# A two-block transformer kernel: the first RMS norm summed in token columns, constants fetched ahead of the weights, and thirty products of zeros at the start

## What is computed

```python
def rms_norm(x, g):
    xf = x.astype(jnp.float32)
    y = xf * lax.rsqrt(jnp.mean(xf * xf, axis=-1, keepdims=True) + EPS)
    return (y * g.astype(jnp.float32)).astype(x.dtype)

def conv_mixers(h, w_in, ...):
    proj = jnp.einsum('bsd,dc->bsc', h, w_in)      # 1024 -> 7168 columns
    ...

x = x + conv_mixers(rms_norm(x, norm_mix_g[l]), w_in[l], ...)
mem_n = rms_norm(mem, norm_mem_g[l])
x = x + memory_cross_attention(rms_norm(x, norm_xa_g[l]), mem_n, ...)
x = x + peer_ffn(rms_norm(x, norm_peer_g[l]), ...)
```

## Time and profile before

| | before |
|---|---|
| time, median of 3 runs | 1473.1 us (1471.33 to 1473.85) |
| time of the profiled execution | 1473.38 us |
| span of the profiled execution (first to last instruction) | 1471.5 us |
| PE busy in the span | 1317.9 us (90%) |
| DVE busy | 955.8 us (65%) |
| ACT busy | 497.2 us (34%) |
| POOL busy | 496.9 us (34%) |
| bytes moved | 397.43 MB, mean 270 GB/s |

### The profile page before, as it was taken

How to read it: one execution, slowest core, us unless ns; L and a number is a source line. 1 busy time by engine, 2 the same in 40 slices (tenths; PEclk the granted TensorE clock), 3 DMA queues, 4 the chain that set the end, 5 groups by cost and what they waited for, 6 DMA issues and landing times.

```text
span 1471.5 us, 25626 instructions
## 1 busy us (share of the span) xinstructions
PE 1317.9 (90%) x9926; PEld 1253.8 (85%) x9926; DVE 955.8 (65%) x2100; ACT 497.2 (34%) x974; POOL 496.9 (34%) x334
## 2 busy tenths in 40 slices
PE   6999999999998886887878886888899999989997
PEld 5999999989888886887868886878776889889997
DVE  4679987665658685859585859655325447683574
ACT  4633456444133121212112121211236455434341
POOL 1588722000224554453535353555012000022221
PEclk9999999999999999898999898999999999999998
DMA  6555554553488999999999999999830125245451
GB/s 244 212 188 185 176 187 166 184 177 154 165 343 329 426 427 427 428 427 427 428 426 426 426 427 427 427 428 427 337 143 29 58 86 194 94 157 199 160 191 40
DMA packets 58090, 397.43 MB, mean 270 GB/s; under 512 B 6288, under 2 KB 9872, under 8 KB 10384
## 3 DMA queue, kind: packets, MB, share of 16 engines
q0 software_dynamic: 36864, 268.45, 43.6%
q1 hardware_dynamic: 21136, 127.76, 24.3%
HBM read 395.14 MB, written 1.05 MB: 269 GB/s over the span
## 4 chain that ended last, share of the span: by engine, by line
PE 55%; DMA 20%; DVE 14%; issue 7%; ACT 3%; POOL 1%; DVEq 0%; POOLq 0%; ACTq 0%
DMA rows_late<-peer_uv_dram,stage 20%; PE bank L721 10%; PE bank L723 10%; PE bank L722 10%; PE bank L963 7%; PE bank L689 6%; PE bank L707 5%; DVE rows_late L1990 4%; ACT w_hi L1165 2%; PE bank L838 1%; DVE w_lo L524 1%; DVE hid L2174 1%; PE bank L862 1%; DVE probs L1916 1%; DVE probs L1914 1%
## 5 line engine op out<-in xcount | busy, mean ns | idle before, releaser
L963 PE MATMUL bank<-h_norm,rows_late 128*128 128x128 f32 x2816 | 329.2, 280 | 24.8 <-ACT h_norm L1352 24.8
L963 PEld LDWEIGHTS bank<-h_norm,rows_late 128*128 128x128 f32 x2816 | 325.6, 196 | 27.8 <-ACT h_norm L1352 27.8
L524 POOL TENSOR_TENSOR w_lo<-raw,w_hi 128x2048 fp32r<-128x2048 f32 x37 | 172.1, 4652 | 392.7 <-ACT w_hi L1165 392.7
L1990 DVE SCALAR_TENSOR_TENSOR rows_late<-rows_late,squares 128x1024 f32<-128x1024 f32 x176 | 213.5, 1229 | 121.1 <-DMA rows_late<-peer_uv_dram,stage 120.6
L963 PE MATMUL bank<-h_norm,rows_early 128*128 128x128 f32 x1280 | 171.9, 300 | 84.7 <-ACT h_norm L1352 84.7
L963 PEld LDWEIGHTS bank<-h_norm,rows_early 128*128 128x128 f32 x1280 | 166.0, 214 | 90.6 <-ACT h_norm L1352 90.5
L631 POOL DMA_INDIRECT rows_late<-peer_uv_dram,stage x165 | 196.4, 1190 | 133.1 <-PE bank L963 94.5
L1165 ACT ACTIVATE w_hi<-raw 128x2048 fp32r<-128x2048 f32 x94 | 178.9, 1904 | 60.4 <-PE bank L723 49.4
L524 DVE TENSOR_TENSOR w_lo<-raw,w_hi 128x2048 fp32r<-128x2048 f32 x57 | 133.0, 2336 | 100.1 <-ACT w_hi L1165 96.5
L721 PE MATMUL bank<-x_hi_a,w_hi 128*128 128x256 f32 x672 | 190.9, 284 | 2.7 <-DVE x_lo_a L1560 1.8
L722 PE MATMUL bank<-x_lo_a,w_hi 128*128 128x256 f32 x672 | 190.2, 283 | 0.0
(11 more groups left out here) (338 smaller groups left out, 2036.5 us busy)
## 6 DMA issues: line engine op xcount, KB each, us to landing
raw<-w_in_dram SPq DMA_DIRECT2D x28, 1024.0 KB, 4.9
raw<-w_up_dram SPq DMA_DIRECT2D x16, 1024.0 KB, 4.9
raw<-w_down_dram SPq DMA_DIRECT2D x16, 1024.0 KB, 4.9
rows_late<-w_in_dram SPq DMA_DIRECT2D x10, 1024.0 KB, 13.4
raw<-w_kv_dram SPq DMA_DIRECT2D x8, 1024.0 KB, 4.8
rows_late<-w_peer_q_dram SPq DMA_DIRECT2D x5, 1024.0 KB, 12.0
raw<-sc_w_out_dram SPq DMA_DIRECT2D x4, 1024.0 KB, 4.8
raw<-cf_w_pw_dram SPq DMA_DIRECT2D x4, 1024.0 KB, 4.8
```

The source lines that it names most:

```text
L524: api.tensor_tensor(ring(w_lo, i), ring(raw, i), ring(w_hi, i).bitcast(F32), ALU.subtract).then_inc(w_lo_ready[LO_BY[i][0]], 1)
L963: mm = nc.tensor.matmul(ct(Y_ACC[c][t // 4], t % 4, P), expert_rows(k)[:, D + t * P:D + (t + 1) * P], ct(diag, k % DIAGS, P), start=False, ...
L1990: w_.scalar_tensor_tensor(out=row, in0=row, scalar=1.0, in1=h_tok[:, c * D:(c + 1) * D], op0=ALU.mult, op1=ALU.mult, accum_out=pre[:, side ...
```

## The change

Five edits, all at the front:

1. The norm "mix" joins `BY_TOKEN`, and its entry in `SUMMED` becomes 1: DVE adds nothing up, PE takes the 8 tiles of squares as they come, in 16 products with one moving column, and `spread("mix")` with its 2 products follows, behind a wait for the constants.
2. The constants are fetched ahead of weight block 0.
3. Weight block 2 is fetched directly behind block 1, ahead of the memory input, the positions and the subkeys.
4. PE begins with `WARM` = 30 products of `zeros` with `zeros`, as soon as POOL's second fill is done.
5. ACT takes a root of one number ahead of the squares, into a place that nothing reads.

The chain of DVE's seven additions for this norm is gone; the reciprocal of 128x256 becomes one of 128x2.

```diff
+WARM = 30
...
-BY_TOKEN = ("peer", "post_mix", "post_mlp")
-SUMMED = {name: DT - 2 if name in ("peer", "post_mix", "post_mlp") else DT for name, _ in NORMS if name != "mlp"}
+BY_TOKEN = ("mix", "peer", "post_mix", "post_mlp")
+SUMMED = {name: 1 if name == "mix" else DT - 2 if name in ("peer", "post_mix", "post_mlp") else DT for name, _ in NORMS if name != "mlp"}
...
             sp.dma_start(vec[:], T["vecs"]).then_inc(vec_landed, 16)
+            sp.dma_start(const[:], T["consts"]).then_inc(const_landed, 16)
             load(0)
             load(1)
-            sp.dma_start(const[:], T["consts"]).then_inc(const_landed, 16)
+            load(2)
...
-            for i in range(2, QUERIES[RING]):
+            for i in range(RING, QUERIES[RING]):
                 load(i)
...
                 for k in tiles:
-                    if k:
+                    if k or SUMMED[name] == 1:
                         pe.wait_ge(squared, square_count(name, k))
...
+            pe.wait_ge(filled, 2)
+            for _ in range(WARM):
+                nc.tensor.matmul(TAP_ACC[0][:, 0:P], zeros[:], zeros[:], start=True, stop=True)
             pe.wait_ge(filled, 4)
             stat_sum("mix")
+            pe.wait_ge(const_landed, 16)
+            spread("mix")
             for b in range(4):
...
+            act.wait_ge(filled, 6)
+            s.activation(sink_e[:, 0:1], eps[:, 0:1], ACT.Sqrt)
             square("mix", lambda k: act.wait_ge(x_landed[k // 4], 16), x_res)
...
-            for k in range(DT):
-                add_to_sum("mix", k)
             dve.wait_ge(vec_landed, 16)
             norm("mix", x_res, "norm_mix_g", h_norm)
```

## The result

The changed kernel takes **1476.76 us** (median of 9 runs, 1474.97 to 1481.37) against 1473.85 of the kernel before (9 runs, 1470.41 to 1474.73); the ratio is **1.0032, 95% interval 1.0023 to 1.0041**. That is 3.4 to 6.0 us slower, small and clear. (The two medians by themselves are 2.9 us apart, and two later sessions gave ratios of 1.0018 and 1.0026, so the size is less sure than the direction.) The time lies in the range of the prediction, but above its forecast of 1474.6 and on the side that it gave a chance of 0.15.

What follows compares the result with a forecast made beforehand. The front's serial chain and TensorE's clock in the 32 plain products were taken as the bound: +1.6 - 0.1 = +1.5 us, 1474.9 against the profiled execution, so 1474.6 against the median; range 1471.2 to 1477.2.

Steps and rivals of the forecast that it cites:

- The zeros: Start of PE's queue: thirty products of zeros end at 10.1 us, costing the sums 2 to 3 us of waiting.
- Sums, root, spread: Norm at the front: sums take 3.6 us; root, reciprocal, spread and first normed tile 2.15, without a table load.
- Rival 5: ACT at the front: the early root fails and a table loads again, +1.3 us to each case; chance 0.01.
- rival 3: Front: zeros do not raise the clock, sums take 7.0 us, +9.2, total 1482.3 us; chance 0.02.
- The fall between: Between zeros and plain products: the clock falls at 13.5 us, costing the last sums 0.2 and the spread 0.4.
- Rival 1: Front: the clock holds because the sums count as work; start +1.1, plain products -2.24, total 1471.9 us; chance 0.30.
- First plain product: End of the front: the first plain product starts at 16.4 us, 1.6 later than 14.77.
- Plain products: The 32 plain products: low clock for 4.4 us against 4.60 before, so 0.1 us less.
- The transfers: Order of weight, constant and memory loads: all delays covered, gain or loss nothing; 3 us at most if covers were gone.
- The step that failed: From 31 to 240 us PE is busy 208.69 of 209.00, so a front shift was taken to move everything later.
- Same: Verdict: the measurement cannot be told from no change, between 1470.2 and 1476.0 us; chance 0.79.
- Rival 2: Front: low clock lasts long at both places and falls early; +4.0, total 1477.1 us; chance 0.12.

Runs made afterwards that it cites:

- r2: The changed kernel with nothing altered, run and profiled again for another front and more runs; ratio 1.0026 (1.0014 to 1.0037) to the kernel before.
- r1: The changed kernel with nothing altered, run again for a second profile and more runs; ratio 1.0018 (1.0005 to 1.0031) to the kernel before.
- r3: The changed kernel with nothing altered, profiled a fourth time; a single run, profiled span 1473.8 us.

## Why the prediction was right or wrong

- *The zeros, right in mechanism and size.* Forecast end 10.1, sums at their heels; measured start of the sums 10.54, 10.77, 9.68 and 9.58. The wait for them was put at 2 to 3 us and was 3.2 in the first profile.
- *Sums, root, spread: right.* The sums took 3.6 us where the clock held through them (r2: 3.63) and 4.17 where it fell within them. No table load at the root. Rival 5 is out, and so is rival 3, that zeros do not raise the clock: it rose at 6.62.
- *The fall between, right in kind; its date in part luck.* It came at 13.45 against 13.5 forecast, but in r1 to r3 at 13.94, 15.06 and 14.87, twice behind the sums instead of within them. Wide sums show that the one moving column is what lets it come. Rival 1, in which the sums count as work, is out for narrow sums and would be right for wide ones. The Trainium skill (TensorE: Matmul & The Clock Gate, "Why this matters for your kernels") advises against long idle gaps between bursts of products, so that the clock stays up; this trace shows that their absence is not enough, since the clock fell with PE busy 2.89 of 2.89 us.
- *First plain product*: forecast 16.4, measured 17.34, 17.35, 15.44 and 15.34. The mean is 16.4, but no profile is near it, so that the first one alone would have looked 0.9 off: the agreement is luck. *Plain products*: forecast 0.1 us less; their lengths were 15.15, 15.39, 15.20 and 15.15 against 15.97, 15.79, 15.58 and 16.00, mean 0.6 less. The term was mis-sized: low time of 4.4 us was put in, and 2.93 to 3.42 were measured. So the front came to +0.9 in the mean instead of +1.5.
- *The transfers: right*, nothing.
- **The step that failed** is "what the front gains or loses shifts the whole kernel, the later waits for other engines and for the expert rows with it". It held to 0.2 us up to peer's first plain product, through 340 us of work. It failed at peer, where the clock falls of itself: the low stretch there lasts 6.83 us instead of 3.41 and costs 1.3 us more, which is more than the front. The prediction gave the clock's later low stretches no term and no reason for leaving them out. The one at peer is tied to the front, and it was against the change in all four profiles; the short low time at the front, a gain of 0.6 us, goes together with it. In the table the stretch counts +1.65, because the first profile of the kernel before lacks the pause named below the table; behind it come +1.1 us whose cause stays open.
- *The verdict.* With that the sum is 0.9 + 0.1 + 1.65 + 0.8 + 0.3 = 3.75 us where 1.5 were forecast, just past the 2.9 us that I had called measurable. Of these, 0.9 + 0.1 + 1.3 = 2.3 us are traced to a place and a cause, and 1.45 are not. "Same" at 0.79 was too sure: with a forecast at half that bound and only +-1.5 allowed around it, 2 us left out were enough. Rival 2 had the size (+4.0), but as one front with everything against it; the real one has a mild front and a long low stretch at peer.

## What to carry to other kernels

Products that only warm the clock must be done before the real operand is ready: here the sums stood behind them in PE's queue until 10.54, although the squares were done at 7.36. What fills the time until the real burst should be wide: here six of the eight tiles added up by DVE, 18 products of zeros timed to end with that sum, and three in each gap, turned a loss of 0.3% into a gain of 0.3%, of which the zeros made 3.4 us (0.9991 to 0.9968). That is no guarantee: in one profile the clock fell at the front in spite of them. Sums with one moving column took as long as sums with 128 (3.63 and 3.74 us for 32 records) and didn't hold the clock; let another engine add up first, or give them equal columns. When the front moves by a us or two, look at every later place where TensorE pauses, for the low stretch there can double (3.41 to 6.83 us here), and profile both kernels several times before a difference is assigned.

## What was not expected of the hardware

- TensorE's clock fell to its low level while the engine was busy in every us, with products of 128x128 stationary and one moving column, 29 records in 2.89 us (10.55 to 13.44) in the first profile, and again in r1. With 128 moving columns, 32 records in 3.74 us, it held.
- Products of zeros with zeros raise the clock: at 6.62, 7.11, 4.82 and 4.62 us, with PE at work from 1.13 on.
- A shorter low stretch at the front (2.93 to 3.42 us) came with a longer one 340 us later (6.83 instead of 3.41), in 13 profiles without an exception, and from the clock's rise at the front to its fall at peer all of them have the same 351.57 us.
- The granted clock reads 1.00 in a profile's first us whatever the level: in the changed kernel's first window below it does so beside 16 records in 3.37 us, the spacing of the low level, and the later window has 35 in 3.78.

```profile
1.13:4.50 3.37, 3.37 (x16) 1.00 0.72 236
6.62:10.40 3.78, 3.78 (x35) 1.00 1.02 406
```
